# Second attention of a two-block transformer kernel in another order: differential heads first, other PSUM banks, gates with room of their own, small first transfers

## The chip, the cores and the metric

The kernel is one launch on one core of a Trainium2 chip. The core has five engines with a queue of instructions each: TensorE (PE in the profile, with its weight loads as PEld), VectorE (DVE), ScalarE (ACT), GpSimd (POOL) and SyncE (SP), which here issues all DMA transfers. They meet only at semaphores: an instruction that waits holds up all behind it on its engine. The metric is the device time of one launch in microseconds (us), the median of several runs.

## What is computed

One sequence of 512 tokens with 1024 features goes through two blocks, all in float32. The first block (convolution, stick-breaking attention, feed-forward) is before the part that changes, except for its very start. Of the second block this matters:

```python
h = rms_norm(x, norm_g)
proj = einsum('bsd,de->bse', h, w_in)
mq, mk, mv, mg, dq, dk, dv, dg = split(proj, ...)      # 512 columns each
# moba: 8 heads of 64; with 512 tokens and blocks of 256 every allowed block is chosen, so causal attention
mq, mk = rms_norm(mq, moba_q_norm), rms_norm(mk, moba_k_norm)
m_out = softmax(mq mk^T / 8 - slope * distance, causal) mv  * silu(mg)
# differential: 4 heads, each with two query and key halves of 64 and values of 128
dq, dk = rms_norm(dq, diff_q_norm), rms_norm(dk, diff_k_norm)
a = softmax(dq1 dk1^T / 8 - slope * distance) - lam * softmax(dq2 dk2^T / 8 - slope * distance)
d_out = rms_norm(a dv, diff_subln) * (1 - 0.2) * silu(dg)
x = x + concat(m_out, d_out) @ w_out
```

## The kernel before, in words

Activations lie transposed, 128 features (partitions) by 512 tokens, eight such chunks for 1024 features. Every product of two matrices is made of three fp32r matmuls (`products`, L384 to L386): each operand is split into a high part (a rounded copy, made by ACT) and a low part (the rest, a subtraction made by POOL or DVE), and high*high, high*low and low*high are added in PSUM. I call such three matmuls a triple. The weights come as a stream of 160 units of 128x1024 (512 KB): SP loads a unit into one of four buffers `w_raw`, ACT makes `w_hi` (two buffers), POOL makes `w_lo`, PE multiplies (`unit_tile`: eight triples of 512 columns), DVE reads the PSUM bank out. Semaphores count units (`hi_ready`, `lo_ready`, `units_done`) and tiles read out (`tile_drained`).

Start (L331 to L341, L780 on): SP loads the constants `vec` (224 KB), `x` in two halves of 1 MB, then units 0 to 3. ACT splits four chunks of x, units 0 and 1, then the other four chunks; POOL makes the low parts of units 0 and 1; the first matmul of PE waits for the low part of unit 0.

Second block, in order of time: queries and keys (16 units); the sums of squares per head (L634, 16 matmuls); the first half of the values (four units, `token_tiles`, in PSUM banks 0 to 3); the 16 rows of norms, spread over partitions by PE (L646, L647: two matmuls each with 32 rows, in banks 6 and 7) and multiplied into `y_qk` by DVE (L1388); the other half of the values; then the attention in eight rounds `c`, of which PE, ACT, DVE and POOL each have their own function: `attention_round`, `act_round`, `dve_round`, `pool_round`. Even rounds hold two moba heads, odd rounds one differential head with its two halves. Rounds 1 to 6 run as a loop over pairs (one differential, one moba round). Each round needs, for each of its two heads or halves:

- scores on PE (`scores2`, banks 2 to 4), the bias added and the row maximum taken by DVE (`biased`, L1417, after `bias_h`, L1098) into `s`;
- exponentials on ACT (L1010), the division by their sum on DVE (`normalised`: L1098, for the second half of a differential head L1440, which also subtracts it from the first half);
- the transposition on PE (L678, bank 5 on), a high part on ACT (L1019), a low part on DVE (L1106), the product with the values on PE (`values2`, bank 1). A moba round has two of these, a differential round one, so a pair of rounds has four heads of scores and three of the rest;
- one of eight gate units (`gate_half`, bank 0), read out and clamped by DVE (L1102, L1098), sigmoid on ACT, product on POOL (L1689). There is one buffer `gate`, one `gate_e` and one `att2`. A differential round also takes a root of its mean square (`root` on DVE, after a sum on PE, L727).

The output projection (units `U_W2`, eight tiles, 64 triples) begins when seven of eight rounds have left their result in `b_hi` and `b_lo` (`mixed_ready`). SP loads its units 2 on only after `mixed_ready` has reached eight. The constants of the norm rows (`sel_f`, `sel_t`) are built by POOL after the sums of squares.

## Time and profile before

| | us |
|---|---|
| median of 3 runs | 1253.88 |
| lowest and highest | 1251.0, 1256.47 |
| the profiled execution | 1252.36 |
| its span, first to last instruction | 1250.6 |
| PE, DVE, ACT, POOL busy | 1116.5, 625.4, 446.7, 509.9 |
| first matmul starts | 14.26 |
| second block, first half of the values | 944.5 to 966.5 |
| norm rows | 966.5 to 984.0 |
| other half of the values | 984.0 to 1007.8 |
| first transposition of the attention ends | 1030.2 |
| one pair of rounds | 1053.1 to 1097.5 |
| output projection goes on to its end | 1206.8 to 1250.6 |

Every time of day below is from the start of the span. Busy shares of the whole say little here: the stretches have different limits, so the table by stretches is read first, then the waits inside of one pair of rounds.

### The profile page before, as it was taken

The page shows a single profiled execution, that of the slowest core. Times are in us where ns is not written, and L with a number is a line of the kernel's source. Part 1 is how long each engine was busy: PE and PEld are TensorE (multiplying, and loading weights), DVE is VectorE, ACT ScalarE, POOL GpSimd, SP SyncE. Part 2 cuts the span into 40 slices and gives each one's busy share as a digit, 9 for nine tenths or more (in the row PEclk, how much of TensorE's full clock was granted, in tenths as well). Part 3 has the DMA queues.
Part 4 walks back from the last instruction along what each step waited for, and adds up shares of the span by engine and source line. Part 5 has one row for each costly group of instructions (what it writes and reads, how often), then busy time and mean ns, then how long its engine had stood idle before and what let it go on. Part 6 is the DMA issues. An engine that isn't in the chain of part 4 may idle for free.

```text
span 1250.6 us, 14828 instructions
## 1 busy us (share of the span) xinstructions
PE 1116.5 (89%) x4976; PEld 905.8 (72%) x4976; DVE 625.4 (50%) x996; ACT 446.7 (36%) x673; POOL 509.9 (41%) x305
## 2 busy tenths in 40 slices
PE   5999999988498978999999999978999968788788
PEld 4887778777377856888888888857866656666667
DVE  5389689789433273333344200054113336977831
ACT  4222536545443243233233322243222033645521
POOL 3443356347033423444444444432335133454543
PEclk9999989899699978999999999979999768889899
DMA  5223111011014222223222232321231000000022
GB/s 192 86 99 101 51 51 50 34 50 50 17 51 155 97 68 68 84 101 101 88 96 101 100 101 101 115 86 42 94 101 50 17 34 18 18 34 17 17 85 83
DMA packets 24800, 90.84 MB, mean 73 GB/s; under 512 B 2752, under 2 KB 2880, under 8 KB 24384
## 3 DMA queue, kind: packets, MB, share of 16 engines
q1 hardware_dynamic: 24768, 90.42, 21.1%
q8 instruction: 19, 0.31, 0.1%
q14 instruction: 13, 0.11, 0.0%
HBM read 88.31 MB, written 2.10 MB: 72 GB/s over the span
## 4 chain that ended last, share of the span: by engine, by line
PE 70%; issue 13%; POOL 7%; DVE 5%; ACT 3%; DMA 1%; DVEq 0%; POOLq 0%; SPq 0%; ACTq 0%
PE ps L384 23%; PE ps L385 22%; PE ps L386 21%; POOL w_lo L1542 3%; POOL pa_lo L1595 2%; DVE s L1440 1%; PE ps L678 1%; DVE s L1417 1%; POOL sp_lo L1590 1%; PE ps L634 1%; PE ps L646 1%; DMA w_raw<-weights 1%; ACT s L1010 0%; PE ps L647 0%; POOL k_lo L1669 0%
## 5 line engine op out<-in xcount | busy, mean ns | idle before, releaser
L1542 POOL TENSOR_TENSOR w_lo<-w_raw,w_hi 128x1024 fp32r<-128x1024 f32 (+1 forms) x140 | 334.4, 2390 | 496.6 <-ACT w_hi L754 449.1
L754 ACT ACTIVATE w_hi<-w_raw 128x1024 fp32r<-128x1024 f32 x136 | 142.1, 1045 | 375.5 <-PE ps L386 374.1
L384 PE MATMUL ps<-a_hi,w_hi 128*128 128x512 f32 x496 | 205.3, 414 | 27.8 <-POOL w_lo L1542 17.9
L384 PE MATMUL ps<-b_hi,w_hi 128*128 128x512 f32 x464 | 185.0, 399 | 26.8 <-POOL w_lo L1542 8.7
L385 PE MATMUL ps<-a_lo,w_hi 128*128 128x512 f32 x496 | 200.2, 404 | 0.0
L386 PE MATMUL ps<-a_hi,w_lo 128*128 128x512 f32 x496 | 199.5, 402 | 0.0
L385 PE MATMUL ps<-b_lo,w_hi 128*128 128x512 f32 x464 | 183.0, 394 | 0.0
L386 PE MATMUL ps<-b_hi,w_lo 128*128 128x512 f32 x464 | 182.9, 394 | 0.0
L384 PEld LDWEIGHTS ps<-a_hi,w_hi 128*128 128x128 f32 x496 | 98.5, 199 | 50.3 <-issue 29.6
L384 PEld LDWEIGHTS ps<-b_hi,w_hi 128*128 128x128 f32 x464 | 88.9, 192 | 49.3 <-issue 20.6
L386 PEld LDWEIGHTS ps<-a_hi,w_lo 128*128 128x128 f32 x496 | 97.4, 196 | 21.8
L385 PEld LDWEIGHTS ps<-a_lo,w_hi 128*128 128x128 f32 x496 | 98.1, 198 | 19.5
L386 PEld LDWEIGHTS ps<-b_hi,w_lo 128*128 128x128 f32 x464 | 88.5, 191 | 18.9
L385 PEld LDWEIGHTS ps<-b_lo,w_hi 128*128 128x128 f32 x464 | 88.9, 192 | 18.2
L1201 DVE SCALAR_TENSOR_TENSOR conv_acc<-u_pad,vec,conv_acc x60 | 73.8, 1230 | 0.0
L1658 POOL TENSOR_TENSOR w_lo<-w_raw,w_hi 128x1024 fp32r<-128x1024 f32 x16 | 38.6, 2410 | 85.4 <-ACT w_hi L985 66.5
L384 PE MATMUL ps<-h_hi,w_hi 128*128 128x512 f32 x176 | 68.5, 389 | 0.0
L385 PE MATMUL ps<-h_lo,w_hi 128*128 128x512 f32 x176 | 68.5, 389 | 0.0
L386 PE MATMUL ps<-h_hi,w_lo 128*128 128x512 f32 x176 | 68.5, 389 | 0.0
L1102 DVE TENSOR_TENSOR up_h<-up_u,up_s 128x512 f32<-128x512 f32 x22 | 48.1, 2184 | 21.1 <-ACT up_s L932 21.0
L1102 DVE TENSOR_TENSOR up_u<-ps,scale_row 128x512 f32<-128x512 f32 x22 | 15.2, 690 | 86.5 <-PE ps L386 86.5
L1102 DVE TENSOR_TENSOR sq_f<-sq_f 128x512 f32<-128x512 f32 x14 | 9.7, 692 | 97.3 <-ACT sq_f L951 96.3
(265 smaller groups left out, 1897.2 us busy)
## 6 DMA issues: line engine op xcount, KB each, us to landing
w_raw<-weights SPq DMA_DIRECT2D x160, 512.0 KB, 3.3
resid<-x_t SPq DMA_DIRECT2D x2, 1024.0 KB, 6.4
resid<-x_t SPq DMA_DIRECT2D x1, 2048.0 KB, 8.6
out_t<-out_sb SPq DMA_DIRECT2D x8, 256.0 KB, 2.0
vec<-vecs SPq DMA_DIRECT2D x1, 224.0 KB, 2.5
```

The costliest lines, as they stand in the source:

```text
L384: pe.matmul(out, s_hi, m_hi, start=first, stop=False, skip_group_check=True)
L385: pe.matmul(out, s_hi, m_lo, start=False, stop=False, skip_group_check=True)
L386: return pe.matmul(out, s_lo, m_hi, start=False, stop=last, skip_group_check=True)
L634: mm = pe.matmul(ps[0:32, 4, :], head_sel[:, 30 - 2 * j:62 - 2 * j], sq_q[:, j, :], start=j == 0, stop=j == 15)
L646: pe.matmul(ps[:, 6 + j % 2, :], sel_t[:, j, :], rows_hi[:, :], start=True, stop=False)
L678: mm = pe.transpose(psf[:, o:o + P], s2[:, head, src:src + P], ident[:, :])
L754: act.activation(w_hi[:, k % 2, 0:width], w_raw[:, k, 0:width], ACT.Copy).then_inc(hi_ready, 1)
L1102: return dve.tensor_tensor(out, in0, in1, op)
L1201: V.do(dve.scalar_tensor_tensor(out=acc if k == TAPS - 1 else dst, in0=src, scalar=w, in1=dst, op0=ALU.mult, op1=ALU.add))
L1542: pool.tensor_tensor(w_lo[:, k % 2, 0:width], w_raw[:, k, 0:width], w_hi[:, k % 2, 0:width].bitcast(F32), ALU.subtract).then_inc(lo_ready, 1)
L1595: pool.tensor_tensor(pa_lo[:, w], pa[:, w], pa_hi[:, w].bitcast(F32), ALU.subtract).then_inc(pal_ready, 1)
L1658: pool.tensor_tensor(w_lo[:, m % 2, :], w_raw[:, slot, :], w_hi[:, m % 2, :].bitcast(F32), ALU.subtract).then_inc(lo_ready, 1)
```

## The change

1. Rounds are all written out (no loops), the even ones now differential and the odd ones moba; each engine's work is put in one list over a pair `c`, `c + 1`, in which pieces of three heads alternate. The values of the differential heads are computed first.
2. PSUM: attention output bank 0, transposed weights banks 1 to 3, scores banks 4 to 6, gate bank 7.
3. `gate_g` and `gate_e` have a chunk for each of eight rounds (in `b_lo` and `b_hi`), `att2` has two. The clamp of the gate moves from DVE to POOL.
4. The norm rows lie between the token blocks of the second half of the values, the scores of round 0 after its fifth and seventh chunk.
5. The first two tiles of the output projection are multiplied, as far as their first six chunks go, in the last pair; its units come through the ordinary stream.
6. `x` comes in eight transfers, unit 0 in two; DVE makes the low part of unit 0. Most of `vec` comes last.
7. `sel_t` and `dist` are built earlier on POOL, and the scalar lambda before the second block.

Of the lists by which the rounds run on PE, ACT and DVE, the diff below shows the new lines alone; what they replace are the functions of the rounds and their loops, printed above. DVE's list is shown from the biasing of `c + 2` on; ahead of it in a pair stand `slopes(c + 1, 1)`, `normalised(c + 1, 0)`, `biased(c + 1, 1)`, `slopes(c + 2)`, `gate_drain(c)` and `raw_out(c)`. POOL's list of a pair is, in this order: gate unit `c`, `stage_v(c - 1)`, `mixed_low(c - 3)`, `gate_clamp(c - 2)`, `stage_qk(c + 1)`, `gate_silu(c - 2)`, `gate_clamp(c - 1)`, gate unit `c + 1`, `gated_out(c - 2)`, `gate_silu(c - 1)`, `mixed_low(c - 2)`, `stage_v(c)`, `stage_qk(c + 2)`.

```diff
-            sp_eng.dma_start(vec[:, :], vecs).then_inc(vec_loaded, 16)
-            for n in range(2):
-                sp_eng.dma_start(resid[:, 4 * n:4 * n + 4, :], xT[:, 4 * n:4 * n + 4, :]).then_inc(x_loaded[n], 16)
-            for k in range(4):
+            def load_x(c):
+                sp_eng.dma_start(resid[:, c, :], xT[:, c, :]).then_inc(x_loaded[c], 16)
+            sp_eng.dma_start(vec[:, 0:KC], vecs[:, 0:KC]).then_inc(gain_loaded, 16)
+            load_x(0)
+            sp_eng.dma_start(w_raw[:, 0, 0:UNIT // 2], wstream[0][:, 0:UNIT // 2]).then_inc(half_loaded, 16)
+            load_x(1)
+            load_x(2)
+            sp_eng.dma_start(w_raw[:, 0, UNIT // 2:], wstream[0][:, UNIT // 2:]).then_inc(raw_loaded[0], 16)
+            for c in range(3, KC):
+                load_x(c)
+            for k in range(1, 4):
                 sp_eng.dma_start(w_raw[:, k, :], wstream[k]).then_inc(raw_loaded[k], 16)
+            sp_eng.dma_start(vec[:, KC:], vecs[:, KC:]).then_inc(vec_loaded, 16)
...
-            with sp_eng.Fori(U_WO // 4 + 1, U_G2 // 4) as n4:
+            with sp_eng.Fori(U_WO // 4 + 1, UNITS // 4) as n4:
                 load(n4)
...
-            for k in range(4):
-                pe.wait_ge(tile_drained, k + 1)
-                unit_tile(k, k % 2, k, a_hi, a_lo, fresh=0 if k == 0 else None)
+            for c in range(KC):
+                pe.wait_ge(split_lo, c + 1)
+                if c % 4 == 0:
+                    pe.wait_ge(half_lo, c // 4 + 1)
+                w = slice(c * P, (c + 1) * P)
+                mm = products(ps[:, 0, :], w_hi[:, 0, w], w_lo[:, 0, w], a_hi[:, c, :], a_lo[:, c, :],
+                              first=c == 0, last=c == KC - 1)
+            mm.then_inc(units_done, 1)
...
+            def value_piece(u0, n, rows=False):
+                u, kk = n // 2, n % 2
...
+                    if kk and b == TB - 1:
+                        mm.then_inc(units_done, 1)
+                    if rows:
+                        norm_row(4 * n + b)
...
+            def norm_row(n):
+                if n >= 2:
+                    pe.wait_ge(nb_used, n - 1)
+                j, bank = NORM_ORDER[n], 6 + n % 2
+                pe.matmul(ps[:, bank, :], sel_t[:, j, :], rows_hi[:, :], start=True, stop=False)
+                pe.matmul(ps[:, bank, :], sel_t[:, j, :], rows_lo[:, :], start=False, stop=True).then_inc(nb_ready, 1)
...
+            pe.wait_ge(tile_drained, CREDIT + T_V2 + 4)
+            for n in range(KC):
+                value_piece(U_V2 + 4, n, rows=n < 4)
+                if n == 4:
+                    pe.wait_ge(nb_used, 16)
+                    scores2(0, 0)
+                if n == 6:
+                    scores2(0, 1)
+            gate_half(0, 0)
+            scores2(1, 0)
+            transposes(0)
+            for c in range(0, KC, 2):
+                more = c + 2 < KC
+                gate_half(c, 1)
+                scores2(c + 1, 1)
+                values2(c)
+                transposes(c + 1, 0)
                 if more:
+                    scores2(c + 2, 0)
+                gate_half(c + 1, 0)
+                square_sum(c)
                 if more:
+                    scores2(c + 2, 1)
+                gate_half(c + 1, 1)
+                transposes(c + 1, 1)
+                if not more:
+                    pe.wait_ge(tile_drained, CREDIT + T_W2)
+                    pe.wait_ge(lo_ready, U_W2 + 1)
+                    out_chunks(0, 0, KC - 2)
+                values2(c + 1, 0)
+                if more:
+                    gate_half(c + 2, 0)
+                    scores2(c + 3, 0)
                 else:
+                    pe.wait_ge(s2_biased, 4 * 16)
+                    pe.wait_ge(lo_ready, U_W2 + 2)
+                    out_chunks(1, 0, KC - 2)
+                values2(c + 1, 1)
+                if more:
+                    transposes(c + 2)
+            out_chunks(0, KC - 2, KC)
+            out_chunks(1, KC - 2, KC)
+            pe.wait_ge(out_read, KC)
+            for t in range(2, KC):
+                pe.wait_ge(lo_ready, U_W2 + t + 1)
+                out_chunks(t, 0, KC)
...
+                more = c + 2 < KC
+                if c:
+                    high_probs(c - 1, 1)
+                split_unit(U_G2 + c + 1)
+                if c:
+                    exponentials(c, 1)
+                    gate_sigmoid(c - 1)
+                    stage_v(c)
+                    high_mixed(c - 2)
+                high_probs(c)
+                exponentials(c + 1, 0)
                 if more:
+                    stage_qk(c + 2)
+                if c:
+                    high_mixed(c - 1)
+                stage_v(c + 1)
+                split_unit(U_G2 + c + 2)
+                exponentials(c + 1, 1)
+                square_out(c)
+                high_probs(c + 1, 0)
                 if more:
+                    exponentials(c + 2, 0)
+                    stage_qk(c + 3)
+                gate_sigmoid(c)
+                first_root(c)
+            high_probs(KC - 1, 1)
...
             for c in range(KC):
                 dve.wait_ge(split_hi, c + 1)
                 low_scaled(a_lo[:, c, :], resid[:, c, :], col("g_mix_pre", c), a_hi[:, c, :]).then_inc(split_lo, 1)
+                if c in (0, 2):
+                    half_low(c // 2)
             for c in range(1, KC):
...
+            def biased(c, head):
+                hd = 2 * c + head
+                V.wait()
+                dve.wait_ge(s2_ready, hd + 1)
+                if c:
+                    dve.wait_ge(pt_ready, tq_of(c - 1, head) + 1)
                 V.do(dve.memset(small[:, 24:25], 0.0))
                 for b in (3, 2, 0, 1):
                     w = slice(S_COL[b], S_COL[b] + (b + 1) * P)
+                    dve.tensor_tensor_reduce(out=s2[:, head, w], in0=psf[:, S_BANK * 512 + w.start:S_BANK * 512 + w.stop],
...
+                    normalised(c + 2, 0)
+                variance(c)
+                gate_drain(c + 1)
+                if more:
+                    biased(c + 2, 1)
+                    root(c)
+                low_probs(c + 1, 1)
+                if more:
+                    normalised(c + 2, 1)
+                    slopes(c + 3, 0)
+                    biased(c + 3, 0)
+                else:
+                    root(c)
+                gated(c + 1)
+                if more:
+                    low_probs(c + 2)
...
+            pool.wait_ge(units_done, U_DN)
+            pool.memset(sel_f[:, :, :], 0.0).then_inc(pool_step, 1)
...
+            def gate_clamp(c):
+                j = chunk_of(c)
+                pool.wait_ge(tile_drained, CREDIT + T_G2 + c + 1)
+                pool.tensor_scalar(gate_e[:, j, :], gate_g[:, j, :], -80.0, None, ALU.max).then_inc(gate_clamped, 1)
...
```

The order of the instructions at three places. SP at the start, before (`resid` is x, `w_raw` the weights):

```order
L331 DMA vec<-vecs 128x448
L333 DMA resid<-x_t 128x2048 x2
L335 DMA w_raw<-weights 128x1024 x4
L345 UNCONDITIONAL_BRANCH
L345 ISA
```

and with the change:

```order
L341 DMA vec<-vecs 128x8
L339 DMA resid<-x_t 128x512
L343 DMA w_raw<-weights 128x512
L339 DMA resid<-x_t 128x512 x2
L346 DMA w_raw<-weights 128x512
L339 DMA resid<-x_t 128x512 x5
L350 DMA w_raw<-weights 128x1024 x3
L351 DMA vec<-vecs 128x440
```

Half of unit 0 now comes behind one chunk of x, and the bulk of `vec` behind unit 3.

PE at the norm rows, before (`sel_t` and `rows_hi`, `rows_lo` are the norm rows, `w_hi`, `a_hi` the values):

```order
L646 MATMUL ps<-rows_hi,sel_t 128x512
L647 MATMUL ps<-rows_lo,sel_t 128x512
L646 MATMUL ps<-rows_hi,sel_t 128x512
L647 MATMUL ps<-rows_lo,sel_t 128x512
L646 MATMUL ps<-rows_hi,sel_t 128x512
L647 MATMUL ps<-rows_lo,sel_t 128x512
```

and with the change:

```order
L378 MATMUL ps<-w_hi,a_hi 128x512
L379 MATMUL ps<-w_lo,a_hi 128x512
L380 MATMUL ps<-w_hi,a_lo 128x512
L656 MATMUL ps<-rows_hi,sel_t 128x512
L657 MATMUL ps<-rows_lo,sel_t 128x512
L378 MATMUL ps<-w_hi,a_hi 128x512
L379 MATMUL ps<-w_lo,a_hi 128x512
L380 MATMUL ps<-w_hi,a_lo 128x512
L656 MATMUL ps<-rows_hi,sel_t 128x512
L657 MATMUL ps<-rows_lo,sel_t 128x512
```

The 16 rows have moved from a block of their own into the first 16 token blocks of the second half of the values.

DVE around the division of a differential head, before (`s_135` holds the weights, `pt_lo` the low part of the transposed weights):

```order
L1106 TENSOR_TENSOR pt_lo<-ps,pt_hi 128x1280
L1102 TENSOR_TENSOR gate<-ps,scale_row 128x512
L1098 TENSOR_SCALAR gate_e<-gate 128x512
L1427 RECIPROCAL rden<-den 128x4
L1098 TENSOR_SCALAR rden<-rden,small 128x4
L1440 SCALAR_TENSOR_TENSOR s_135<-s_135,rden 128x512
L1440 SCALAR_TENSOR_TENSOR s_135<-s_135,rden 128x384
L1440 SCALAR_TENSOR_TENSOR s_135<-s_135,rden 128x128
L1440 SCALAR_TENSOR_TENSOR s_135<-s_135,rden 128x256
L1524 UNCONDITIONAL_BRANCH
L1524 ISA
L1106 TENSOR_TENSOR pt_lo<-ps,pt_hi 128x1280
```

and with the change, from the same division on:

```order
L1489 SCALAR_TENSOR_TENSOR s_134<-s_134,rden 128x256
L1141 TENSOR_SCALAR bias_h<-dist,small 128x512
L1463 MEMSET small 128x1
L1466 ISA s_134,smax<-ps,bias_h 128x512
L1466 ISA smax 128x1
L1466 ISA s_134,smax<-ps,bias_h 128x384
L1466 ISA smax 128x1
L1466 ISA s_134,smax<-ps,bias_h 128x128
L1466 ISA smax 128x1
L1466 ISA s_134,smax<-ps,bias_h 128x256
L1466 ISA smax 128x1
L1141 TENSOR_SCALAR neg_max<-smax 128x4
```

Behind those, with the change, come the gated output of the moba round before (`att_127`) and then `pt_lo`. The clamp `gate_e<-gate` is gone from DVE, and between the division and the low part of the same head there is now the biasing of the next one.

## Rows read from the trace of the kernel before

**Rows 1.** The page, chain of work that ended last, shares of the span.

```profile
PE 70%; issue 13%; POOL 7%; DVE 5%; ACT 3%; DMA 1%; DVEq 0%; POOLq 0%; SPq 0%; ACTq 0%
```

**Rows 2.** Busy time by stretch; columns named in the first row.

```profile
core 0: us, PE busy (x) PEld busy (x) DVE busy (x) ACT busy (x) POOL busy (x), PEclk, DMA share, GB/s
966.50:984.00 17.50, 15.15 (x33) 7.18 (x32) 13.80 (x19) 1.06 (x1) 2.35 (x1) 0.63 0.19 61
1004.60:1030.20 25.60, 13.31 (x50) 11.23 (x50) 10.71 (x35) 9.39 (x23) 7.55 (x8) 0.64 0.12 42
1053.10:1097.50 44.40, 35.80 (x166) 29.70 (x165) 35.33 (x81) 24.17 (x54) 20.78 (x22) 0.85 0.07 25
1030.20:1206.80 176.60, 140.22 (x644) 115.30 (x643) 131.64 (x294) 90.28 (x196) 79.78 (x79) 0.87 0.05 18
```

**Rows 3.** Timeline of the start: start, duration, engine, line, operation, [idle before <-releaser].

```profile
6.73 2.56 ACT L784 ACTIVATE a_hi<-resid,vec 128x512 fp32r<-128x512 f32 x4 [4.56 <-DMA resid<-x_t]
...
10.44 1.06 ACT L754 ACTIVATE w_hi<-w_raw 128x1024 fp32r<-128x1024 f32 x1 [1.16 <-DMA w_raw<-weights]
...
14.26 0.77 PE L384 MATMUL ps<-a_hi,w_hi 128*128 128x512 f32 x1 [14.26 <-POOL w_lo L1542]
...
18.94 0.39 PE L386 MATMUL ps<-a_hi,w_lo 128*128 128x512 f32 x1
...
27.37 0.95 PE L421 MATMUL ps<-ones,sq_x 128*128 128x1 f32 x8
```

**Rows 4.** Timeline of DVE and PE before the second block's queries, POOL's constants.

```profile
866.93 3.87 DVE L1102 TENSOR_TENSOR y_qk<-ps,scale_row 128x512 f32<-128x512 f32 x6
873.60 0.77 PE L384 MATMUL ps<-a_hi,w_hi 128*128 128x512 f32 x1 [3.66 <-POOL w_lo L1542]
945.20 1.80 POOL L1640 MEMSET sel_f<- 32x2048 f32 x1
...
949.74 1.89 POOL L1651 CAST sel_t<-sel_f 32x2048 fp32r<-32x2048 f32 x1
```

**Rows 5.** Timeline of DVE and PE at the norm rows.

```profile
966.64 2.72 DVE L1098 TENSOR_SCALAR v_tok<-ps,ncol 128x512 f32<-128x512 f32 x4 [3.77 <-PE ps L386]
970.08 0.50 PE L646 MATMUL ps<-rows_hi,sel_t 32*128 32x512 f32 x1 [2.35 <-DVE y_qk L1388]
```

**Rows 6.** Timeline of DVE in the pair of rounds from 1053.1.

```profile
1066.82 1.27 DVE L1098 TENSOR_SCALAR s<-s,rden 128x512 f32<-128x512 f32 x4
...
1070.01 4.52 DVE L1098 TENSOR_SCALAR s<-s,rden 128x512 f32<-128x512 f32 x4
...
1083.92 2.38 DVE L1098 TENSOR_SCALAR s<-s,rden 128x512 f32<-128x512 f32 x4
...
1091.39 5.05 DVE L1440 SCALAR_TENSOR_TENSOR s<-s,rden 128x512 f32<-128x512 f32 x4
```

**Rows 7.** Groups by shape in that pair (count | busy, mean ns | idle before).

```profile
L1106 DVE TENSOR_TENSOR pt_lo<-ps,pt_hi 128x1280 fp32r<-128x1280 f32 x3 | 4.5, 1489 | 4.4 <-ACT pt_hi L1019 4.4
L1440 DVE SCALAR_TENSOR_TENSOR s<-s,rden 128x512 f32<-128x512 f32 x1 | 0.8, 753 | 0.0
L1689 POOL TENSOR_TENSOR gate_e<-gate,gate_e 128x512 f32<-128x512 f32 x2 | 2.6, 1278 | 0.0
```

**Rows 8.** Timeline of PE: the first scores and transpositions, and values in the pair.

```profile
1014.72 0.76 PE L384 MATMUL ps<-k_hi,q_hi 64*128 64x512 f32 x1 [6.75 <-POOL k_lo L1669]
...
1028.00 2.40 PE L678 MATMUL ps<-ident,s 128*128 128x128 f32 x10 [3.56 <-DVE s L1098]
...
1060.22 0.50 PE L384 MATMUL ps<-pt_hi,v_hi 128*128 128x512 f32 x1
...
1062.36 0.50 PE L384 MATMUL ps<-k_hi,q_hi 64*128 64x512 f32 x1
```

**Rows 9.** Timeline of the output projection: PE, and the last read-out on DVE.

```profile
1206.81 0.80 PE L384 MATMUL ps<-b_hi,w_hi 128*128 128x512 f32 x1 [4.62 <-POOL b_lo L1669]
...
1247.51 0.69 DVE L1102 TENSOR_TENSOR out_sb<-ps,resid 128x512 f32 x1 [4.75 <-PE ps L386]
```

681 lines of the change are left out of this document (319 added, 362 removed).

## The prediction

> **What bounds the kernel now.** I read the chain of waits first: PE carries 70% of it, so over the whole the kernel is PE's [rows 1]. The table by stretches says where it is not. In the norm rows PE runs at a granted clock of 0.63, on the way to the first transposition of the attention it is busy 13.3 of 25.6 us, and through the attention 140 of 176.6 us at 0.87 [rows 2]. At full clock the work is less than PE's busy time there. A triple of 512 columns costs 0.68 us (37 matmuls from 18.94 to 27.37, 0.228 each, [rows 3]) and a head of scores or values 2.14 [rows 8]; the transposition of one head is 2.4 at the clock of a PE that has waited [rows 8], and I take 1.1 at full. A pair of rounds is 16 triples (10.9), four heads of scores and three of values (15.0), three transpositions (3.3) and one sum (0.9): 30 us, where the pair takes 44.4. DVE is busy 35.3 of the same 44.4 [rows 2]. So a pair is a ring in which PE and DVE wait for one another in turn; neither is full, and the floor of an ideal order is DVE's 35, not PE's 30.
>
> **The sum** is made against the profiled execution: span 1250.6, time 1252.36, so 1.8 lie outside; the median of the runs, 1253.88, is 1.5 above that execution.
>
> **1, the start.** The first matmul waits until 14.26 for the low part of unit 0, whose data ACT takes up at 10.44, behind 2.2 MB of `vec` and x; the first half of x is in at 6.73 [rows 3]. With the change 4 KB, 256 KB of x and 256 KB of weights come first. 1.2 MB took until 6.7 and 2.7 MB until 10.4, so 1.5 MB cost 3.7 us, 0.6 us for 256 KB; the first two pieces should be in at about 4.5, and ACT and DVE need some 1.5 for both high and low part: PE starts at 6. The remaining chunks arrive every 0.65 to 0.8 us, faster than a triple at half clock (1.28) and about as fast as one at full. The first tile so ends near 13.3. The second does not start there: unit 1 arrives as late as before (about 11.5), ACT takes 1.06 and POOL 2.5, so 15.2, and 5.4 for eight triples give 20.6 instead of 27.2. Gain 6.0; 4.5 if the wait of 2 us sets the clock back, 7 if unit 1 comes earlier. What is late next is unit 2, whose split now follows the eight squares on ACT: ready at 20.4, just in time. DVE's two half subtractions (0.7 each) are hidden by the arrival of x; without that cover they would cost 1.4.
>
> **2, constants.** POOL's steps for `sel_t` and `dist` run from 945.20 to 951.63 [rows 4]; without the 0.6 of `dist`, 5.8 us are those of `sel_t`. They now follow the low part of the second down-projection unit, and the third unit's low part waits for them: 3.5 (split and low part of the second) + 5.8 + 2.4 = 11.7 against two units of PE, 10.9. Cost 0.8, and 0 to 2 as bounds. In front of the queries PE waits 3.66 until 873.60 for a weight unit which ACT takes after four squares, and these wait for DVE's read-out at 866.93 [rows 4]; lambda's steps, 1.7 us, no longer stand there. Gain 1.7. Both together: gain 0.9.
>
> **3, values and norm rows.** Before, 63.8 us lie between the end of the first half of the values (966.4) and the end of the first transposition (1030.2). Now: PE waits for DVE's four read-outs of the first half, 2.9 us (2.72 in [rows 5]); the rows covered it before. Then 32 triples (21.8), 16 rows of two matmuls (7.3 at 0.228 each) and two heads of scores (4.3). Before, a wait of 2.35 us at this place [rows 5] was followed by rows at a clock of 0.63 [rows 2]; now rows of 32 partitions alternate with full matmuls, so I expect half clock for a few us: 3 us extra (bounds 1 and 8, if the rows held it down). The last piece ends at 966.4 + 39.3 = 1005.7. PE then waits for four more read-outs (2.8) while DVE, not PE, has the longest list: read-outs 2.8, division of the two halves 3 and 3.9 (between 1.27 and 4.5, and between 2.1 and 5, [rows 6]), then the transposition 1.6: 1017.0. Gate and scores of the next round hide in it. Gain 13.2, of which the merging of the rows is about two thirds. Bounds 8 and 16.
>
> **4, the pairs.** DVE's list loses two clamps (0.85); nothing else leaves it. Its idle time of 9.1 in a pair of 44.4 [rows 2] came from waits for its own head's next step, 4.4 of it ahead of the low parts [rows 7]; now another head's work stands in each of these places. I followed one pair from the end of `transposes(c)`, with the durations of [rows 6 to 8] and, of the same timeline, 1.9 for a head's biasing, 2.3 for its exponentials on ACT and 1.2 for a high part: scores of `c + 1` biased and its exponentials out by 4.4, `values2(c)` done at 7, first scores of `c + 2` biased at 13.7, `square_sum` at 15.3, the second at 23.2 (DVE waits 0.4 for the transposition of the moba head that shares the buffer), root to 26.0, low part to 27.4, and the differential division to 32.2; then the transposition: 34. The one wait left is there: `biased(c + 3, 0)` must not write `s` before `transposes(c + 2)` has read it, and `gated` and `low_probs` queue behind it on DVE. I add 1.5 to 2 for signal times left out at some fifteen changes of engine: 36 a pair. The gate's clamp costs nothing on POOL, at the price of the nearest product there, 1.28 [rows 7], since POOL is busy 20.8 of 44.4 [rows 2]; bounds 0.4 and 2.6. From the end of the first transposition: three pairs of 36, and the last one to the point where its last result is split. There DVE has no new scores; the chain is `high_probs` behind `values2(7, 0)`, low part at 26.3, root to 29.2, gate product on POOL, split on ACT, low parts on POOL: 34.2. Together 142.2 against 176.6 [rows 2]: gain 34.4.
>
> **5, the projection.** 51 of 64 triples are left then, 34.7 us, plus 2 for the clock after a wait of some 3 us (before: 4.62, [rows 9]), 0.3 to DVE's read-out, 0.7 for it and 2.4 from its end (1248.2) to the end of the span [rows 9]: 40.1. Before it was 43.8 (1206.8 to 1250.6), with 57 triples and units that came late. Gain 3.7. The 13 triples done earlier lie where PE would wait.
>
> Sum: 6.0 + 0.9 + 13.2 + 34.4 + 3.7 = 58.2; the span becomes 1192.4, the time 1194.2, and a median like that of the runs 1195.7. I say **1196**.
>
> **Rivals.** *Shared ports.* The same DVE instructions take very different times: the division of a head 1.27, 4.52 and 2.38, that of a differential head 5.05 where its first part alone is 0.75 and the four some 2.1 [rows 6, 7]. In sum 7.3 us of DVE's 35.3 are such excess, and the slow ones lie where POOL works. If it grows with POOL's share, from 20.8/44.4 to (20.8 + 2.6)/36, it becomes 10.1: a pair of 38.8, 2.8 more, and +10 in 3.6 pairs; I double this for collisions that lie worse, up to 41.6 a pair: 1206 to 1216, at **1208**. [...]
>
> *The ring keeps its pace.* If the wait for the transposition behind the differential division drags PE's next gate and scores with it at half clock, a pair stays at 44: +8 in 3.6 pairs, **1225**. For it: the clock falls after each such wait. Against: the new lists leave one such place in a pair.
>
> *Contention falls instead.* If the alternation happens to put POOL's work under DVE's PSUM reads, a pair is 32: **1182**.
>
> *Heads in series, slower than before.* With in-order queues one misplaced wait makes every head run alone. The first two heads of the attention do that now: 13.3 us from first scores to transposition, after a wait of 6.75 for POOL's low part [rows 8]. A pair would be 2 x (13.3 + 3.8) + 3 x 7.2 (transposition, high part, low part, values) = 56, 20 more than forecast, and four pairs +79: **1275**. It decides from 50 a pair on. Against it: in the hand-followed pair every wait on another engine ends before or within 2 us of the moment at which the waiting engine arrives.
>
> *The start does nothing.* If small transfers take as long as large ones, PE starts at 14 as before: +6, within the range.
>
> **Chances.** Forecast (34.5 to 38 a pair, 1187 to 1203) 0.60; ports 0.20; 32 a pair or less 0.09; old pace 0.07; a pace near 49 that ends at no change 0.01; in series 0.03. Differences under 0.5% (6 us) are about what a measurement of this kernel cannot tell from none. Range **1182 to 1216**: the forecast, the ports and half of the case below, 0.84. Faster 0.96, same 0.01, slower 0.03.
>
> **What would show it.** Start: first matmul near 6 and the first sum of squares near 20.8 instead of 27.37. Rows: end of the second half of the values about 39 after the first, with a granted clock over 0.85. Pairs: 36 from one differential transposition to the next, DVE busy over 90%, and the same excess of some 7 in its divisions; an excess of 10 or more means the ports. Projection: 35 to 37 of PE without waits at the end. The forecast is wrong if DVE shows waits of over 2 us at more than one place in a pair, or if PE runs at half clock for more than a quarter of it.

## The result, and the profile of the changed kernel

| | before | changed |
|---|---|---|
| median, lowest and highest (us) | 1252.71, 1251.0, 1256.47 | 1233.91, 1232.35, 1235.2 |
| span of the profiled execution | 1250.6 | 1230.6 |
| ratio | | 0.985, 95% interval 0.983 to 0.987 |

The change is faster by 18.8 us where 58 were forecast, and the time lies above the upper end of the range, 1216. Cut at the same points as the sum of the prediction, the two traces say where:

| step | forecast gain (us) | measured | missed |
|---|---|---|---|
| 1, start (as left in the middle of the program) | 6.0 | 2.1 | 3.9 |
| 2, constants | 0.9 | -0.9 | 1.8 |
| 3, values and norm rows | 13.2 | -12.2 | 25.4 |
| 4, pairs | 34.4 | 29.6 | 4.8 |
| 5, projection | 3.7 | 1.5 | 2.2 |

The sum of the measured gains is 20.1, the spans differ by 20.0. Step 3 carries two thirds of what is missing. Steps 3 to 5 are lengths inside a trace. Steps 1 and 2 compare times of day in one execution of each kernel, and these move between executions by more than the two gains (below), so they are rough. The table by stretches of the changed kernel shows it (us, then busy us and count of PE, PEld, DVE, ACT and POOL, then granted clock, DMA share, GB/s). In the clock column 1.00 is the full clock of PE and 0.50 the half clock: at 1.00 one matmul of 512 columns starts 0.23 us after the last (976.04 and 976.27 in `bank_wait`), at 0.50 it starts 0.43 after it (990.40 and 990.83 here). Its lines answer to [rows 2]:

```profile
965.30:968.40 3.10, 0.16 (x1) 0.00 (x0) 2.73 (x4) 1.20 (x2) 1.71 (x1) 1.00 0.37 139
968.40:1011.70 43.30, 43.22 (x81) 20.99 (x81) 11.26 (x15) 3.75 (x5) 7.16 (x8) 0.51 0.07 25
1011.70:1029.90 18.20, 18.17 (x72) 13.99 (x72) 6.59 (x22) 4.07 (x12) 4.77 (x2) 0.86 0.18 59
1029.90:1041.30 11.40, 8.01 (x35) 6.25 (x36) 10.31 (x16) 3.45 (x9) 5.49 (x5) 0.85 0.15 46
1041.30:1075.70 34.40, 31.88 (x165) 26.50 (x165) 29.89 (x78) 23.88 (x53) 19.45 (x19) 0.95 0.10 32
1075.70:1113.20 37.50, 33.77 (x166) 27.79 (x165) 32.45 (x79) 24.39 (x54) 23.43 (x24) 0.91 0.09 29
1113.20:1149.00 35.80, 31.71 (x165) 26.23 (x164) 32.74 (x79) 24.52 (x54) 27.23 (x26) 0.97 0.09 30
1149.00:1188.30 39.30, 31.30 (x146) 24.75 (x145) 22.23 (x47) 17.73 (x34) 17.47 (x15) 0.94 0.08 27
1188.30:1230.60 42.30, 36.81 (x153) 29.68 (x153) 5.54 (x8) 6.36 (x6) 14.28 (x6) 0.96 0.22 75
```

The second line is the stretch with the 16 norm rows among the value blocks. PE is busy all of its 43.3 us, and its clock is 0.51. A busy engine at half clock looks full in a table of busy shares; only the column of the clock shows it. The three lines from 1041.3 to 1149.0 are the pairs: 34.4, 37.5 and 35.8, where 36 each was forecast.

### The profile page after: what moved, and what is told of

The parts are those of the page before. It is cut to its first block, busy times and chain, and to the rows that moved or that the text cites. A ratio compares the mean times of both kernels' runs of the same rounds, so it can differ in the third digit from the quotient of the medians.

```text
span 1230.6 us, 14513 instructions
## 1 busy us (share of the span) xinstructions
PE 1125.2 (91%) x4976; PEld 899.3 (73%) x4976; DVE 617.9 (50%) x989; ACT 446.3 (36%) x673; POOL 518.5 (42%) x312
## 4 chain that ended last, share of the span: by engine, by line
PE 55%; issue 24%; POOL 13%; DVE 5%; ACT 2%; DMA 0%; POOLq 0%; SPq 0%; DVEq 0%; ACTq 0%
PE ps L378 18%; PE ps L379 16%; PE ps L380 16%; POOL w_lo L1590 9%; POOL pa_lo L1646 2%; POOL sp_lo L1641 1%; PE ps L632 1%; PE ps L685 1%; PE ps L656 1%; DVE s L1141 1%; DVE s L1489 1%; DVE v_tok L1141 1%; PE ps L657 1%; DVE s L1466 0%; DVE att L1537 0%
## 5 line engine op out<-in xcount | busy, mean ns | idle before, releaser
L1590 POOL TENSOR_TENSOR w_lo<-w_raw,w_hi 128x1024 fp32r<-128x1024 f32 x155 | 370.1, 2389 | 559.5 <-ACT w_hi L796 512.1
L796 ACT ACTIVATE w_hi<-w_raw 128x1024 fp32r<-128x1024 f32 (+1 forms) x151 | 157.9, 1046 | 403.0 <-PE ps L380 402.4
L1145 DVE TENSOR_TENSOR up_u<-ps,scale_row 128x512 f32<-128x512 f32 x22 | 15.2, 690 | 86.5 <-PE ps L380 86.5
L1641 POOL TENSOR_TENSOR sp_lo<-sp,sp_hi 128x896 fp32r<-128x896 f32 (+1 forms) x16 | 27.6, 1735 | 73.3 <-ACT sp_hi L878 73.3
```

The lines of the kernel that those rows point to most:

```text
L796: act.activation(w_hi[:, k % 2, 0:width], w_raw[:, k, 0:width], ACT.Copy).then_inc(hi_ready, 1)
L1145: return dve.tensor_tensor(out, in0, in1, op)
L1590: pool.tensor_tensor(w_lo[:, k % 2, 0:width], w_raw[:, k, 0:width], w_hi[:, k % 2, 0:width].bitcast(F32), ALU.subtract).then_inc(lo_ready, 1)
L1641: pool.tensor_tensor(sp_lo[:, w], sp[:, w], sp_hi[:, w].bitcast(F32), ALU.subtract).then_inc(spl_ready, 1)
```

## The experiments

Times are medians of the runs, to be held against 1233.9 of the changed kernel. Between executions the unchanged part of the program differs by up to 6 us (POOL's first step for the selector starts at 703.1 in one trace and at 709.1 in another), so inside a trace I compare the length of a stretch: from DVE's first read-out of the first half of the values to its first of the second half. It is 64.4 us in the changed kernel (1029.91 - 965.50):

```profile
965.50 2.73 DVE L1141 TENSOR_SCALAR v_tok<-ps,ncol 128x512 f32<-128x512 f32 x4 [13.81 <-PE ps L380]
1029.91 2.73 DVE L1141 TENSOR_SCALAR v_tok<-ps,ncol 128x512 f32<-128x512 f32 x4 [0.87 <-PE ps L380]
```

**Where the rows stand.** Two orders of the same work.

```diff
 rows_block:
+            for n in range(2 * KC):
+                norm_row(n)
             pe.wait_ge(tile_drained, CREDIT + T_V2 + 4)
             for n in range(KC):
-                value_piece(U_V2 + 4, n, rows=n < 4)
+                value_piece(U_V2 + 4, n)
 rows_late:
-                        norm_row(4 * n + b)
+                        norm_row(4 * (n - 2) + b)
...
-                value_piece(U_V2 + 4, n, rows=n < 4)
-                if n == 4:
+                value_piece(U_V2 + 4, n, rows=2 <= n < 6)
+                if n == 5:
```

> The changed kernel, but the 16 normalising matmul pairs of the 32-row selector stand in one block before the second half of the values again, as in the kernel before; the read-outs of the first half are hidden under them and the value pieces have none among them. Theory A (the selector matmuls, on 32 partitions, hold TensorE's granted clock at its lower level wherever they stand, so the mix drew the whole second half of the values to half clock): values and rows take about 24 + 17.5 + 24 = 66 us instead of 76.0, the granted clock in the second half of the values is back near full, and the time is 1215 to 1225. Theory B (the 3 us wait before the mix lowers the clock and the mix itself has no part in it): here no wait, so the same 1215 or so, but then the late rows below would gain at least as much. If neither holds, 1234.

> The changed kernel, but the 16 normalising matmul pairs stand among chunks 2 to 5 of the second half of the values instead of chunks 0 to 3. Theory B (the wait lowers the clock, and it rises again a few us later whatever runs): two chunks of full products let the clock rise before the rows come, and the rest runs at full clock: about 20 us less, 1214. Theory A (the rows themselves keep the clock at half, or bring it down): the clock falls again with the first rows or stays down, and at most 3 to 6 us are gained, 1228 to 1234.

Measured: 1215.9 (ratio to the kernel before 0.970, interval 0.968 to 0.972) and 1219.7 (0.974, 0.972 to 0.975); the stretch is 46.3 and 47.6 us. Neither theory comes out whole. With the rows late, PE waits the same 3.02 us, and this is the table by stretches behind it:

```profile
966.00:970.00 4.00, 1.25 (x4) 1.10 (x5) 2.49 (x4) 1.51 (x2) 2.35 (x1) 0.92 0.18 71
970.00:974.00 4.00, 4.00 (x13) 3.11 (x12) 0.00 (x0) 0.00 (x0) 0.00 (x0) 0.66 0.43 135
974.00:980.00 6.00, 6.00 (x24) 3.68 (x23) 1.50 (x2) 0.21 (x1) 0.00 (x0) 1.00 0.00 0
980.00:992.00 12.00, 12.00 (x40) 6.02 (x39) 5.82 (x8) 2.95 (x4) 8.93 (x8) 1.00 0.17 44
```

The clock falls after the wait (0.66 in 970 to 974), is back at full by 974, and stays there through all 16 rows (1.00 in 976.7 to 1000.3). So these rows did not bring the clock down. In the changed kernel, where they follow the wait at once, it does not rise before they end (0.51 in 968.4 to 1011.7). Behind this wait the clock falls, with or without rows; with the rows right behind it, it stays low. The late rows gain 16.8 us in this stretch and give 3.2 of it back behind it (see **Constants**).

**Why it doesn't rise under the rows.** Width, or short chains between read-outs?

```diff
-        sel_f = place("sel_f", [32, 16, P], F32, at["b_lo"])
-        sel_t = place("sel_t", [32, 16, P], F32R, at["b_lo"] + 4 * 16 * P)
+        sel_f = place("sel_f", [P, 16, P], F32, at["b_lo"])
+        sel_t = place("sel_t", [P, 16, P], F32R, at["b_lo"] + 4 * 16 * P)
...
-        rows_hi = put("rows_hi", [32, T], F32R)
+        rows_hi = put("rows_hi", [P, T], F32R)
...
+            for part in (rows_hi, rows_lo):
+                pool.memset(part[32:64, :].bitcast(F32), 0.0).then_inc(sel_ready, 1)
+                pool.memset(part[64:P, :].bitcast(F32), 0.0).then_inc(sel_ready, 1)
```

> The changed kernel in its order (rows in chunks 0 to 3), but the selector and its two operands have 128 partitions (96 of zeros), so that each normalising matmul is as wide as the others. The runs so far: with the rows in one block the time fell by 18 us, with the rows in chunks 2 to 5 by 14 us, and there the granted clock was back at full before the rows came and stayed there through all of them. So the rows do not bring the clock down; what is open is why it does not rise under them. Theory A (rows of 32 partitions don't let it rise): here it rises about 4 us after the wait at 968.5, and the time is 1210 to 1216. Theory C (the pattern of short chains, whatever their width): no change, 1234.

Measured: 1207.9 (0.963, 0.960 to 0.966); the stretch is 38.6 us, 25.8 less. The order and the wait of 3.02 us are those of the changed kernel; the same table:

```profile
966.00:970.00 4.00, 0.98 (x4) 0.80 (x4) 2.73 (x4) 1.69 (x2) 2.36 (x1) 0.96 0.25 95
970.00:974.00 4.00, 4.00 (x12) 3.10 (x12) 1.46 (x2) 0.00 (x0) 0.00 (x0) 0.61 0.44 135
974.00:980.00 6.00, 6.00 (x28) 4.94 (x27) 3.80 (x6) 1.41 (x3) 4.24 (x6) 1.00 0.00 0
```

The clock is back at full by 974, where with 32 partitions it was still at 0.51 until 1011.7. The order is the same, so the width decides: three quarters of zeros make the program 26 us faster. Short chains are out.

**The wait itself.** Each bank waits for its own read-out.

```diff
                 for b in range(TB):
+                    if u0 == U_V2 + 4 and n == 0:
+                        pe.wait_ge(tile_drained, CREDIT + T_V2 + b + 1)
...
-            pe.wait_ge(tile_drained, CREDIT + T_V2 + 4)
```

> The changed kernel with one wait cut up: the second half of the values waits for each of its four banks to be read out as it comes to it, not for all four before the first. TensorE then stands about 1.0 us at 965.3 instead of 3.02. If a wait of 1 us leaves the granted clock at full, the rows in chunks 0 to 3 find it there and keep it, as the late rows did: the 3.0 us wait is 1.0, the 24 us of half clock are gone, and the time is about 1208. If the clock falls even after the shorter wait, the rows hold it down again: 1232.

Measured: 1210.4 (0.965, 0.962 to 0.968); the stretch is 41.6 us. PE's wait in the timeline (start, us, instruction, idle before it), then the stretches:

```profile
966.42 0.47 PE L378 MATMUL ps<-w_hi,a_hi 128*128 128x512 f32 x1 [0.94 <-DVE v_tok L1142]
```

```profile
966.00:970.00 4.00, 3.58 (x12) 2.04 (x13) 3.32 (x6) 1.27 (x2) 2.38 (x1) 1.00 0.13 50
970.00:974.00 4.00, 4.00 (x14) 1.86 (x13) 1.84 (x3) 1.15 (x2) 2.92 (x5) 1.00 0.41 131
```

After 0.94 us the clock is still at full and stays there (1.00 in 966 to 999). But 41.6 us is more than the 38.6 of the wide rows, which had the longer wait and some half clock. The timelines of the two kernels in the mix, PE and its weight loads (PEld), say why. Narrow rows first:

```profile
975.04 0.50 PE L658 MATMUL ps<-rows_hi,sel_t 32*128 32x512 f32 x1
975.38 0.39 PE L659 MATMUL ps<-rows_lo,sel_t 32*128 32x512 f32 x1
975.70 0.50 PE L378 MATMUL ps<-w_hi,a_hi 128*128 128x512 f32 x1
976.04 0.39 PE L379 MATMUL ps<-w_lo,a_hi 128*128 128x512 f32 x1
976.27 0.40 PE L380 MATMUL ps<-w_hi,a_lo 128*128 128x512 f32 x1
976.60 0.50 PE L658 MATMUL ps<-rows_hi,sel_t 32*128 32x512 f32 x1
```

```profile
975.70 0.19 PEld L378 LDWEIGHTS ps<-w_hi,a_hi 128*128 128x128 f32 x1 [0.36 <-issue]
```

Wide rows:

```profile
974.95 0.39 PE L656 MATMUL ps<-rows_hi,sel_t 128*128 128x512 f32 x1
975.18 0.39 PE L657 MATMUL ps<-rows_lo,sel_t 128*128 128x512 f32 x1
975.40 0.39 PE L378 MATMUL ps<-w_hi,a_hi 128*128 128x512 f32 x1
...
976.08 0.39 PE L656 MATMUL ps<-rows_hi,sel_t 128*128 128x512 f32 x1
```

```profile
975.18 0.19 PEld L378 LDWEIGHTS ps<-w_hi,a_hi 128*128 128x128 f32 x1
```

A row and its block take 976.60 - 975.04 = 1.56 us narrow and 1.13 wide. With wide rows the load for the matmul at 975.40 begins at 975.18, under the one before. With narrow rows the load for the matmul at 975.70 begins at 975.70, and those for the rows at 975.04 and 976.60 begin at 975.04 and 976.59: where the width changes in this mix, the weight load is not hidden. The difference, 0.43 us, is two changes of width in each block, some 0.2 us each. The loads themselves take 0.18 us with 32 partitions and 0.19 with 128. What costs is their place, not their length.

**Does it carry over?** The kernel before, with wide selector and operands only (POOL writes the zeros here too, with four more instructions).

```diff
-        sel_t = put("sel_t", [32, 16, P], F32R)
+        sel_t = put("sel_t", [P, 16, P], F32R)
...
-        rows_hi = put("rows_hi", [32, T], F32R)
+        rows_hi = put("rows_hi", [P, T], F32R)
```

> The kernel before, with one thing changed: the selector and its two operands have 128 partitions (96 of zeros). Its 16 normalising pairs stand in a block of 17.5 us at half clock, behind a wait at 966.6, and its granted clock comes back at 988.0, 4 us after their end. If 32 partitions are what the clock does not rise under, it rises here some 4 us after the wait; the pairs at full clock are then bound by VectorE's reads at 0.75 us (12 us for 16), the block is 14 instead of 17.5, and the values behind it start at full clock: 5 to 6 us less, 1246 to 1247. If the short chains between reads are the cause, whatever their width: 1252.

Measured: 1249.3, ratio 0.998 (0.996 to 0.999), some 3 us. The clock rises with wide rows here too, with less to gain. Of the kernel before, and then with wide rows, whose execution is some 5 us later at this place:

```profile
974.00:978.00 4.00, 4.00 (x9) 1.86 (x9) 2.89 (x5) 0.00 (x0) 0.00 (x0) 0.50 0.02 4
978.00:982.00 4.00, 4.00 (x9) 1.86 (x9) 2.94 (x4) 0.00 (x0) 0.00 (x0) 0.50 0.00 0
```

```profile
974.00:978.00 4.00, 3.00 (x6) 1.71 (x7) 3.11 (x5) 0.00 (x0) 1.10 (x1) 0.62 0.38 131
978.00:982.00 4.00, 3.54 (x11) 1.61 (x10) 3.34 (x5) 0.00 (x0) 0.00 (x0) 0.95 0.02 4
```

The same stretch as above goes from 41.4 to 37.1 us, 4.3 less. Some 1 us of that is lost ahead of it: POOL's four zeroings (955.59 to 957.83) put off its next low part, and PE waits 0.75 us at 960.34 where it did not before; the other 4 us of the 5 are there before the selector is built. PE at full clock then waits for DVE's reads, as expected (busy 3.54 of 4 us at 0.95, a read taking 0.75).

**The start.** The old start in the changed kernel (vectors whole, x in two halves, unit 0 whole, its low part by POOL).

```diff
-            sp_eng.dma_start(vec[:, 0:KC], vecs[:, 0:KC]).then_inc(gain_loaded, 16)
-            load_x(0)
...
+            sp_eng.dma_start(vec[:, :], vecs).then_inc(vec_loaded, 16)
+            for n in range(2):
+                sp_eng.dma_start(resid[:, 4 * n:4 * n + 4, :], xT[:, 4 * n:4 * n + 4, :]).then_inc(x_loaded[n], 16)
```

> The changed kernel with the start of the kernel before: the vectors whole and first, x in two halves of 1 MB, the first weight unit whole, its low part by POOL. The traces of the two kernels show 3.3 us between their first sums and only 2.1 us left of it by the middle of the program. So the forecast's 6.0 us would make this 1240; the reading of the traces makes it 1236; if the small transfers are worth nothing in the end, 1234.

Measured: 1236.3 (0.987, 0.985 to 0.989). The new start is worth some 2.4 us by the medians, not 6; the two intervals touch.

**Constants.** Selector and lambda in stretches where POOL and ACT are idle.

```diff
 act:
-            act.wait_ge(lam_sum, 1)
-            act.activation(small[:, 2:4], small[:, 0:2], ACT.Exp).then_inc(lam_exp, 1)
...
             new_residual(4, 2 * KC + FC, a_hi, "g_2", ...)
+            act.wait_ge(lam_sum, 1)
+            act.activation(small[:, 2:4], small[:, 0:2], ACT.Exp).then_inc(lam_exp, 1)
+            act.preload_act_table(ACT.Sqrt)
```

POOL's four steps for `sel_f` and `sel_t` go from ahead of the down projection to behind those of `dist`, DVE's two last ones for lambda behind the norm of the last residual.

> The changed kernel with the selector built by POOL right after the distances (idle there from 861.2 to 870.9 in the trace of the changed kernel) and lambda's exponential with its two table loads on ACT after the last residual (idle there from 847.2 to 854.1), DVE's part of lambda behind its sums. The trace of the changed kernel shows a wait of 1.82 us at 710.4 and half clock after it, 3.8 us in all against the kernel before: this should give them back, 1230, and no less than 1232 if my reading of that stretch is right; 1234 if the down projection makes up for it later.

Measured: 1234.8, no difference to be seen. Its trace has the gain, though: POOL's `dist` starts at 856.11 (859.88 in the changed kernel; 0.2 of these 3.8 us is there before the selector's place), with the same clock row at 712 to 720 at 1.00 instead of 0.79. They are lost again behind the values. PE's waits and the first transposition there, in the changed kernel and then in this one:

```profile
1032.69 0.50 PE L378 MATMUL ps<-a_hi,w_hi 128*128 128x512 f32 x1 [2.82 <-DVE v_tok L1141]
1039.98 1.31 PE L685 MATMUL ps<-ident,s 128*128 128x128 f32 x10 [0.60 <-DVE s L1489]
1050.00 0.50 PE L378 MATMUL ps<-k_hi,q_hi 64*128 64x512 f32 x1 [0.66 <-POOL k_lo L1710]
```

```profile
1029.38 0.50 PE L378 MATMUL ps<-a_hi,w_hi 128*128 128x512 f32 x1 [2.82 <-DVE v_tok L1142]
1036.68 2.05 PE L685 MATMUL ps<-ident,s 128*128 128x128 f32 x10 [0.59 <-DVE s L1490]
1048.35 0.50 PE L378 MATMUL ps<-k_hi,q_hi 64*128 64x512 f32 x1 [0.68 <-POOL k_lo L1710]
```

The wait is the same, 2.82 us, and so is the way to the transposition. But the transposition takes 2.05 us instead of 1.31, and the next scores stand 11.7 us behind its start instead of 10.0. The clock says why. Three stretches of this kernel and then, for the last of them, the changed kernel at the same place:

```profile
1030.00:1034.00 4.00, 4.00 (x12) 2.79 (x10) 4.00 (x4) 0.04 (x1) 4.00 (x4) 0.57 0.00 0
1034.00:1037.00 3.00, 2.41 (x15) 2.07 (x16) 2.93 (x8) 0.00 (x0) 0.15 (x1) 1.00 0.57 173
1037.00:1041.00 4.00, 4.00 (x17) 3.53 (x15) 2.08 (x12) 1.32 (x2) 0.00 (x0) 0.57 0.00 1
```

```profile
1041.00:1044.00 3.00, 3.00 (x16) 2.21 (x14) 2.51 (x11) 1.77 (x2) 0.00 (x0) 1.00 0.00 0
```

In both the clock falls behind the wait of 2.82 (0.57 in 1030 to 1034 here, 0.72 in 1035 to 1039 in the changed kernel) and comes back. Here it falls a second time behind the wait of 0.59 at 1036.68 (0.57), and a third time behind that of 0.68 at 1048.35 (0.84 in 1048 to 1052, 0.73 in 1052 to 1056); in the changed kernel it stays at full behind 0.60 and 0.66 (1.00 in 1039 to 1054). Each of the two falls costs 1.6 us. From DVE's first read-out of the last values to the first sum of a root it is 25.1 us in the changed kernel and in eight others of this study, but 28.3 here and with the late rows, whose clock falls behind the same two waits. (`four`, below, has another order there and 27.3.) `three`, below, has the constants in the same new places and 25.1. So moving them is not the cause. Why the clock falls behind waits this short in two traces and not in nine stays open; chance in the clock is my guess.

**The last head.** ACT splits the second output unit ahead of the last high probabilities, DVE takes the last root ahead of the last low ones.

```diff
-            high_probs(KC - 1, 1)
             split_unit(U_W2 + 1)
+            high_probs(KC - 1, 1)
...
-                if more:
-                    biased(c + 2, 1)
-                    root(c)
+                if more:
+                    biased(c + 2, 1)
+                root(c)
```

> The changed kernel with ACT splitting the second output unit before it takes the last head's high probabilities (so POOL's low part of it is ready near 1172.3 instead of 1177.6), and DVE taking the last differential head's root before the last low probabilities. The wait of 4.81 us at 1172.9 falls away, the end of it with it: 1229 if nothing takes its place; 1232 if the last head's values then wait for something else for most of that time.

Measured: 1226.9 (0.977, 0.974 to 0.980). From the first root's sum to the first tile of the projection it is 128.4 us instead of 134.3. PE's wait in the changed kernel and the same place now:

```profile
1177.69 0.77 PE L378 MATMUL ps<-b_hi,w_hi 128*128 128x512 f32 x1 [4.81 <-issue]
```

```profile
1179.17 0.47 PE L378 MATMUL ps<-b_hi,w_hi 128*128 128x512 f32 x1 [0.30 <-issue]
1188.36 0.50 PE L378 MATMUL ps<-b_hi,w_hi 128*128 128x512 f32 x1 [2.24 <-POOL b_lo L1708]
```

"issue" hides the cause: the profile names no releaser, but POOL's low part of that unit ended at 1177.6. The profiled execution of `tail` is the slowest of its four (1232.4), some 6 us late already at POOL's selector; the length inside the trace is free of that.

**Together, and one step more.** `three` has the cut-up wait, the places and the last head. `four` adds this:

```diff
                 if half == 0:
-                    pe.wait_ge(tile_drained, CREDIT + T_G2 + c)
+                    if c:
+                        pe.wait_ge(tile_drained, CREDIT + T_G2 + c)
...
+            normalised(0, 0)
             biased(0, 1)
             drain_values(U_V2 + 4, 0)
-            normalised(0, 0)
```

> The changed kernel with the three edits of the runs before together: the wait cut up by banks, the selector and lambda in idle stretches, ACT's and DVE's order at the last head. Alone they gave 23.5 us, 0 (its 3.8 us were there at the first query product, and 3.2 were lost again after the values, where the granted clock fell for longer behind the same 2.82 us wait) and 7. If the loss after the values comes by chance of when the clock falls, 1234 - 23.5 - 3.8 - 7 = 1200; if moving the constants forward always costs it, 1203.

> The kernel with the three edits, and the first head's way out of the values changed: the first gate product no longer waits for the four value read-outs (its bank is another), and DVE scales the first half of the first differential head before it takes up the second half's maxima. There the trace with the wait cut up shows DVE's scaling at 4.86 us beside POOL's work, and at 1.27 us for the next head without it; the transposition waits for it until 1017.2. It should start near 1014.5: 2.8 us less, and some 2 us of half clock behind the 2.82 us wait less: about 5 us under the kernel with three edits, 1195. If the wait only moves to the scores (for POOL's low part of k, ready at 1012.4) and the clock falls there, 1 to 3 us.

Measured: 1202.4 (0.959, 0.953 to 0.964) and 1203.2 (0.961, 0.955 to 0.966). The first comes out near the sum of its parts (1200 by the gains inside the traces, 1204 by the medians of the single runs). The second gains nothing. Its timeline, DVE's scaling of the two halves and then PE's wait and transposition:

```profile
998.18 1.27 DVE L1144 TENSOR_SCALAR s<-s,rden 128x512 f32<-128x512 f32 x4
...
1005.95 5.17 DVE L1492 SCALAR_TENSOR_TENSOR s<-s,rden 128x512 f32<-128x512 f32 x4
...
1007.30 0.50 PE L378 MATMUL ps<-k_hi,q_hi 64*128 64x512 f32 x1 [2.21 <-POOL k_lo L1710]
1011.18 2.39 PE L687 MATMUL ps<-ident,s 128*128 128x128 f32 x10 [0.88 <-DVE s L1492]
```

The first half's scaling is 1.27 us instead of 4.86; POOL is idle under it (from 998.23 to 1004.47). But POOL's work now lies under the second half's, 5.17 instead of 1.94: the excess moved from one instruction to the next. POOL's low parts run beside it, from 1004.62 to 1010.05. Where this division took 1.94 us, POOL was idle (1072.08 in the changed kernel; POOL from 1072.01 to 1075.45). The transposition still starts 1.3 us sooner behind the read-outs (8.8 instead of 10.1), but it takes 2.39 us instead of 1.31: the clock falls behind the wait of 2.21 and is at half from 1008.4 to 1015.2 (0.50), with the wait of 0.88 in it.

**The start of the second tile.** `three`, with DVE taking the low part of unit 1:

```diff
+            dve.wait_ge(half_hi, 3)
+            low(w_lo[:, 1, :], w_raw[:, 1, :], w_hi[:, 1, :]).then_inc(one_lo, 1)
...
-            low_weights(0, 1)
```

> The kernel with three edits (1202.4), and at the start the low part of the second weight unit taken by DVE (0.69 us for 512 columns in this trace, so 1.4 for 1024) instead of POOL (2.36). TensorE waits 2.40 us for it at 14.3 now, and runs at half clock until 19.9 behind that wait. With 1.4 us the wait is shorter by 1.0; if the clock then stays up, as it did behind the 1.0 us wait in the values, 3 us are gained at the first sums (24.1 to 21). If attention 1 gives the same share back as it did before, 1 to 2 us of it reach the end, 1201; if the clock falls all the same, 1202.

Measured: 1199.4 (0.957, 0.956 to 0.959), 3 us less than `three`, whose own interval reaches down to it. PE's wait is 1.27 us instead of 2.40 in the changed kernel (its line first), and the clock stays at full (1.00) from 12 to 20. But the edit is not shown to be the reason. With POOL taking the low part, as in the changed kernel, this wait was 1.72 us in `three`, with the clock at full behind it too, and from 0.80 (`tail`) to 2.48 (`rows_128b`) in the other traces. Against `three` the first sums come 1.3 us sooner (23.42 and 24.75), 0.55 of it by PE's start. Behind them the wait for DVE's squares (1.58 us at 23.4, 1.60 in `three`) is followed by half clock in both, 0.57 in 24 to 28 here and 0.57 in 26 to 30 there. So what the trace shows of the 3 us is about 1:

```profile
16.73 0.79 PE L378 MATMUL ps<-a_hi,w_hi 128*128 128x512 f32 x1 [2.40 <-POOL w_lo L1590]
```

```profile
16.11 0.50 PE L379 MATMUL ps<-a_hi,w_hi 128*128 128x512 f32 x1 [1.27 <-POOLq L1640]
```

**The best kernel.** `three_start` with the wide selector and rows.

> The kernel with three edits and the changed start (1199.4), with selector and operands over 128 partitions (96 of zeros) as well. With the cut-up wait the clock is already at full under the rows, so nothing is left to gain from the clock there. But the traces show a second price of the narrow rows: between full matmuls a block with its row takes 1.56 us at full clock (975.04 to 976.60 in the kernel with the cut-up wait) where the wide rows take 1.14 (974.95 to 976.08): 0.42 each, 6.7 in 16. If that price comes from the change of width, this is 1193; if it was the clock alone, 1199.

Measured: 1192.95 (1190.95 to 1194.61), ratio 0.952, interval 0.950 to 0.954. The stretch is 34.9 us, where `three_start` has 41.6. This settles the second price of the narrow rows, that of the changes of width: the clock was at full before this edit and is after it (1.00 from 964 to 997 in both traces), and the forecast of this run, 1193, was made from the 0.42 us alone.

## Why the prediction was wrong, step by step

**Step 3 is the one that failed**: the term for half clock at the norm rows. The forecast was "half clock for a few us: 3 us extra (bounds 1 and 8, if the rows held it down)". Three things were wrong in it.

- The rows held the clock down for all of their stretch (0.51 in 968.4 to 1011.7). The row for this was in hand: before, the rows ran at 0.63 [rows 2]. I put that down to the wait ahead of them [rows 5] and asked no further why the clock came back only behind their end. The bound of 8 was not worked out either: 16 blocks with their rows are 80 matmuls, at 0.228 us each 18.2 and at half clock, 0.43 each (990.40 to 990.83), 34, so the bound was +16. With 0.228 to half clock, 3 us extra and no price for the change of width I had 21.2 us; it took 43.7 (16 times 2.73), 22.5 more.
- Of these 22.5, 6.7 are the changes of width at full clock (16 times 0.42, `best`). The remaining 15.8 are half clock beyond the 3 allowed. [rows 3] has 0.228 for equal matmuls in a row only.
- By merging the rows the change exposed the wait of 3 us directly ahead of them. I had priced the wait (2.9, measured 3.02), and not what it does to what follows. Cut to 0.94, the same order is 23.5 us faster.

The remaining 2.9 of the 25.4 are half clock that outlasts the rows: from 1011.7 to 1029.9 it took 18.2 us, where the rest of the values and two heads of scores were forecast at 15.2. The way from there to the end of the transposition was right, 11.4 for 11.3.

**Step 4 was right in its sum for the pairs, and in part by luck.** It is 107.7 us for three pairs against 108. The rival of the ports, 38.8 a pair, did not come (no run shows a port; what the traces show is an excess of DVE's divisions beside POOL's work), nor did the old pace, and PE is at half clock for 6 to 18% of a pair (0.91 to 0.97), less than the quarter named as a sign of being wrong. But DVE was to be over 90% busy with the same excess of some 7 us in its divisions, and is at 87 to 91. The excess (over 1.27 a head and 1.94 for the differential one) is 0.3, 1.0 and 4.8 us in the three pairs; most of the difference is in the differential division, one line for each pair. POOL is idle under the first two (1072.01 to 1075.45 and 1109.36 to 1112.60) and works under the third (from 1141.48 on):

```profile
1072.08 1.94 DVE L1489 SCALAR_TENSOR_TENSOR s<-s,rden 128x512 f32<-128x512 f32 x4
1109.42 1.94 DVE L1489 SCALAR_TENSOR_TENSOR s<-s,rden 128x512 f32<-128x512 f32 x4
1141.58 4.95 DVE L1489 SCALAR_TENSOR_TENSOR s<-s,rden 128x512 f32<-128x512 f32 x4
```

So DVE has 29.9 to 32.7 us of work in a pair where I had some 34, and stands still for 3.1 to 5.1, where I allowed some 2 (0.4 for a wait, 1.5 to 2 for signal times). The two errors cancel. Part of "Contention falls instead" came true (the excess of 0.3 and 1.0), without its 32 a pair.

The last pair was mis-sized: 39.3 instead of 34.2. I had followed the chain to the last result and not the second output unit, whose split stands behind `high_probs(7, 1)` on ACT. `tail` gives 5.9 of it back.

**Step 1.** PE starts at 6.8 (6 forecast), but the first tile ends at 14.3 instead of 13.3 and the second starts at 16.7 instead of 15.2, at half clock (0.59 in 16 to 20). The case was named (4.5 "if the wait of 2 us sets the clock back") and not taken. At the first sums 3.3 are gained, 2.1 later on, 2.4 by the run; where the rest goes I did not follow.

**Step 2.** The selector was to cost 0.8; it cost some 3.6, since a wait of 1.82 us is followed by half clock (0.79 in 712 to 720). The half clock is the same omission; the wait itself should have been 0.8. In front of the queries 2.7 are gained where I had 1.7: the wait is 1.90 instead of 3.66, and the half clock behind it is shorter (0.79 in 876 to 878, where it was 0.50).

**Step 5.** 42.3 instead of 40.1: the third unit finds both `w_hi` buffers held by the two half-finished tiles, a wait of 2.32 us that ends at 1192.9 (ACT splits the unit at 1189.34, when PE releases a buffer, and POOL's low part ends at 1192.8). The unfinished tiles fill PE's idle time earlier and pay here.

Steps 1, 2 and 3 share one omission: a wait of 1.8 to 3 us was priced at its length, and the half clock behind it at nothing or too little. It costs some 1.7 us in steps 1 and 2, and some 19 where narrow matmuls follow. Steps 2, 4 and 5 each have a wait besides that was not in the sum, or not at this length (1.82, 4.81 and 2.32 us).

## What to carry to other kernels

Price a wait of TensorE at its length plus the half clock that can follow it (some 1.7 us at each place measured here), and look at what runs next: narrow matmuls (32 partitions here) right behind a wait can keep the engine at half clock for as long as they last (0.51 for 43.3 us here). Pad them to full width with zeros (25.8 us less in the stretch here), or put full ones first (16.8), and wait for each bank by itself (22.8). Do not scatter narrow matmuls among wide ones: here each change of width exposed a weight load and cost some 0.2 us (0.42 for the two of a block). And read the clock column of a stretch in which the engine looks fully busy.
